# Swapping the two operands of the samples' value matmuls in the attention stage of a decoder step

## The reference, cut to what matters

```python
o_cmp = jnp.einsum('bkgtn,bnkd->btkgd', p_cmp, vc.astype(F32))      # 255 compressed blocks
...
o_sel = nsa_selected(qg, k_sel, v_sel, top_idx, top_ok, qpos, rel_bias)  # 16 blocks chosen out of the 4096 past positions
...
o_win = nsa_window(qg, kw_all, ...)                                  # the last 512 positions
...
o = gates[:, :, 0] * o_cmp + gates[:, :, 1] * o_sel + gates[:, :, 2] * o_win
```

## Time and profile before

| | share of the span | instructions |
|---|---|---|
| PE (matmul) | 91% | 13788 |
| PEld (weight load) | 77% | 13788 |
| VectorE | 44% | 2381 |
| ScalarE | 19% | 1184 |
| GpSimd | 11% | 322 |

### The profile page before, as it was taken

The page is one execution under the profiler, slowest core; times in us unless marked ns, Lnnn a source line. Parts: engine busy times, 40 slices in busy tenths (PEclk is TensorE's granted clock), DMA queues, the critical chain, the costliest instruction groups (busy, mean ns, idle before and its releaser), DMA issues. The chain is left out here.

```text
span 2642.2 us, 38209 instructions
## 1 busy us (share of the span) xinstructions
PE 2404.4 (91%) x13788; PEld 2026.4 (77%) x13788; DVE 1167.7 (44%) x2381; ACT 498.3 (19%) x1184; POOL 294.0 (11%) x322
## 2 busy tenths in 40 slices
PE   7996999689798999999989969986988989999997
PEld 6873999567597788888868759985767868888885
DVE  1933665445457544101038246654544675440012
ACT  1013111223421211000010221112342221110001
POOL 0600000000222011001006000000003121110010
PEclk9996999789899999999989979987999989999998
DMA  6204998244210222522042159962440103215210
GB/s 193 80 27 136 266 267 217 67 129 121 73 42 18 80 80 80 144 64 64 0 125 64 32 162 268 263 165 82 139 124 18 42 17 112 80 48 126 65 32 34
DMA packets 335879, 273.89 MB, mean 104 GB/s; under 512 B 53569, under 2 KB 331458, under 8 KB 335482
## 3 DMA queue, kind: packets, MB, share of 16 engines
q1 hardware_dynamic: 272424, 203.30, 27.9%
q10 hardware_dynamic: 63314, 68.70, 9.8%
HBM read 262.07 MB, written 18.17 MB: 106 GB/s over the span
## 5 line engine op out<-in xcount | busy, mean ns | idle before, releaser
L2658 PE MATMUL psum<-ff,HT 128*128 128x272 f32 x1536 | 353.3, 392 | 0.0
L447 PE MATMUL psum<-xT,ring 128*128 128x272 f32 x1408 | 327.5, 396 | 21.5 <-PEq L169 21.5
L2658 PEld LDWEIGHTS psum<-ff,HT 128*128 128x128 f32 x1536 | 291.8, 190 | 60.2
L447 PEld LDWEIGHTS psum<-xT,ring 128*128 128x128 f32 x1408 | 269.9, 192 | 78.1 <-issue 22.0
L1156 DVE STREAM_TRANSPOSE turned<-ring 128x1536 f32<-128x1536 f32 x128 | 222.7, 1765 | 117.6 <-PE psum L1035 78.8
L1035 PE MATMUL psum<-turned,W 128*128 128x128 f32 x2048 | 249.1, 281 | 0.0
L1035 PEld LDWEIGHTS psum<-turned,W 128*128 128x128 f32 x2048 | 241.2, 197 | 0.0
L2504 PE MATMUL psum<-yT,HT 128*128 128x272 f32 x896 | 215.1, 397 | 0.0
L2504 PEld LDWEIGHTS psum<-yT,HT 128*128 128x128 f32 x896 | 172.4, 193 | 36.0
L1025 PE MATMUL psum<-yT,turned 128*128 (+1 forms) x1024 | 123.5, 275 | 32.6 <-DVE turned L1156 32.6
L1025 PEld LDWEIGHTS psum<-yT,turned 128*128 128x128 f32 x1024 | 122.7, 196 | 34.0 <-issue 32.0
(11 more groups left out here) (526 smaller groups left out, 3336.4 us busy)
## 6 DMA issues: line engine op xcount, KB each, us to landing
ring<-in_cache_nsa_kv SPq DMA_DIRECT2D x256, 192.0 KB, 5.5
ring<-in_cache_nsa_kv ACTq DMA_DIRECT2D x256, 192.0 KB, 5.6
ring<-in_w_up SPq DMA_DIRECT2D x32, 1024.0 KB, 5.5
ring<-in_cache_nsa_kv SPq DMA_DIRECT2D x384, 64.0 KB, 1.9
HT<-in_w_down SPq DMA_DIRECT2D x12, 2048.0 KB, 9.0
ring<-in_w_in SPq DMA_DIRECT2D x20, 1024.0 KB, 5.2
ring<-in_cache_nsa_kv ACTq DMA_DIRECT2D x128, 64.0 KB, 2.2
HT<-in_w_out SPq DMA_DIRECT2D x8, 1024.0 KB, 5.2
```

Of the source, the lines that this page charges most:

```text
L447: last = pe.matmul(psum[0:w.shape[1], 2 * (t % 3) + h, 0:HALF], w, S.xT[:, k, h * HALF:(h + 1) * HALF], start=(k == 0), stop=(k == KT - 1))
L2658: last = pe.matmul(out[h], down[t % 3][:, k, :], f[:, k, x], start=(k == 0), stop=(k == FT - 1))
```

## The change

In `sample_third` the two operands of each matmul change places: the values (pages, window, compressed blocks, new tokens) are now stationary, 128 positions by 128 channels, and the 16 columns of probabilities move. The sum has its 128 channels on partitions and a sample's 16 rows as columns, so that all 8 samples fit in 128 columns of bank 7. The copies out of PSUM (L1496), the waits for them (L1419, L1483), the 8 transposes at the end (L1485) and the buffer `o_s` go away. VectorE's placement into `yT` now waits for the last half of the last sample (`s.part`) where it waited for the transposes. The counts of matmuls, and the DMAs, are the same.

```diff
@@ -1364,7 +1364,6 @@
     half = NPG // 2
     vsel = ring_view(S, 2, half, P)
     vwin = sb("vwin", [P, 4, P], ctx=ctx)
-    o_s = sb("o_s", [16, NB, P], ctx=ctx)
     units = [(i, h, br) for i in range(QT) for br in range(3) for h in (0, 2, 1, 3)]
     N = len(units)
     sc = sb("sc", [P, 3, 512], ctx=ctx)
@@ -1374,7 +1373,7 @@
     coef = sb("coef", [P, N], ctx=ctx)
     o = sb("o", [P, QT, 256], ctx=ctx)
     names = ("scored", "added", "step", "maxed", "exped", "turned", "pt_copied", "pv", "summed", "coef", "o_turned", "o_copied",
-             "pages0", "pages1", "pages_act0", "pages_act1", "window", "part", "s_copied", "s_turned", "placed")
+             "pages0", "pages1", "pages_act0", "pages_act1", "window", "part", "placed")
     with stage(nc, "att", *names) as (block, s):
         pages, pages_act = (s.pages0, s.pages1), (s.pages_act0, s.pages_act1)
         by_sp = 12
@@ -1413,23 +1412,21 @@
                 part, third = n // 3, n % 3
                 b, h = part // 2, part % 2
                 cols = slice(16 * b, 16 * b + 16)
-                o = psum[0:16, 6 + b % 2, 0:P]
+                o = psum[:, 7, cols]
                 if h == 0 and third == 0:
-                    if b >= 2:
-                        pe.wait_ge(s.s_copied, b - 1)
-                    pe.matmul(o, S.pt_new[:, 0, cols], S.kv_s[:, 3 * P:4 * P], start=True, stop=False)
-                    pe.matmul(o, S.pt_new[:, 1, cols], S.kv_s[:, 5 * P:6 * P], start=False, stop=False)
+                    pe.matmul(o, S.kv_s[:, 3 * P:4 * P], S.pt_new[:, 0, cols], start=True, stop=False)
+                    pe.matmul(o, S.kv_s[:, 5 * P:6 * P], S.pt_new[:, 1, cols], start=False, stop=False)
                     for j in range(2):
                         m = P - j
-                        pe.matmul(o, S.pt_cmp[0:m, j, cols], S.vc[0:m, j, b, :], start=False, stop=False)
+                        pe.matmul(o, S.vc[0:m, j, b, :], S.pt_cmp[0:m, j, cols], start=False, stop=False)
                     pe.wait_ge(s.window, 16 * b + 16)
                     for j in range(4):
-                        pe.matmul(o, S.st_win[:, j, cols], vwin[:, j, :], start=False, stop=False)
+                        pe.matmul(o, vwin[:, j, :], S.st_win[:, j, cols], start=False, stop=False)
                 if third == 0:
                     pe.wait_ge(pages[h], 16 * by_sp * (b + 1))
                     pe.wait_ge(pages_act[h], 16 * (half - by_sp) * (b + 1))
                 for t in range(half * third // 3, half * (third + 1) // 3):
-                    last = pe.matmul(o, S.st_sel[:, half * h + t, cols], vsel[:, h, t, :], start=False, stop=(h == 1 and t == half - 1))
+                    last = pe.matmul(o, vsel[:, h, t, :], S.st_sel[:, half * h + t, cols], start=False, stop=(h == 1 and t == half - 1))
                 if third == 2:
                     last.then_inc(s.part, 1)
 
@@ -1480,10 +1477,6 @@
             for n in range(N - lag, N):
                 sample_third(n)
             pe.wait_ge(s.summed, N)
-            pe.wait_ge(s.s_copied, NB)
-            for b in range(NB):
-                last = pe.transpose(psum[:, 7, 16 * b:16 * b + 16], o_s[:, b, :], C["ident"][0:16, 0:16])
-            last.then_inc(s.s_turned, 1)
             for i in range(QT):
                 for c in range(2):
                     last = pe.transpose(psum[:, (6, 0)[c], i * P:i * P + P], o[:, i, c * P:c * P + P], C["ident"])
@@ -1491,10 +1484,6 @@
 
         @block.scalar
         def _(act):
-            def copy_out(b):
-                act.wait_ge(s.part, 2 * b + 2)
-                act.copy(o_s[:, b, :], psum[0:16, 6 + b % 2, 0:P]).then_inc(s.s_copied, 1)
-
             def fetch_rest(part):
                 if part >= 2:
                     act.wait_ge(s.part, part - 1)
@@ -1509,8 +1498,6 @@
                     act.wait_ge(s.maxed, n + 1)
                     x = sc[:, n % 3, 0:width(n)]
                     act.activation(x, x, ACT.Exp, bias=nmax[:, n:n + 1], accum_out=esum[:, n:n + 1]).then_inc(s.exped, 1)
-                if n - lag - 2 in range(6, 6 * NB, 6):
-                    copy_out((n - lag - 2) // 6 - 1)
                 if n >= 1:
                     m = n - 1
                     act.wait_ge(s.turned, m + 1)
@@ -1519,8 +1506,6 @@
                     w = 31 if width(m) == 31 else P
                     x = slice(0, P if w == 31 else width(m))
                     act.copy(pt[0:w, m % 3, x], psum[0:w, 2 + m % 2, x]).then_inc(s.pt_copied, 1)
-            for b in range((N - lag - 2) // 6, NB):
-                copy_out(b)
             act.wait_ge(s.o_turned, 1)
             for c in range(2):
                 act.copy(S.yT[:, 4 + c, 0:SEQ], psum[:, (6, 0)[c], :]).then_inc(s.o_copied, 1)
@@ -1559,7 +1544,7 @@
                     else:
                         dve.wait_ge(s.summed, m)
                         dve.scalar_tensor_tensor(out, src, coef[:, m:m + 1], out, ALU.mult, ALU.add).then_inc(s.summed, 1)
-            dve.wait_ge(s.s_turned, 1)
+            dve.wait_ge(s.part, 2 * NB)
             rows = psum[:, 7, 0:P].rearrange("p (b k g t) -> p b k g t", b=NB, k=KVH, g=GRP)
             for k in range(KVH):
                 for g in range(GRP):
```

## The result

The changed kernel takes 2808.96 us, the median of 4 runs (2805.81 to 2821.52), against 2642.7 for the kernel before, now the median of 4. The ratio is 1.0636, with a 95% interval of 1.0614 to 1.0659: 6.4% slower. The profiled execution took 2805.81 us, 161.8 more than that of before. The granted clock is 0.873 on average over the span, where it was 0.946.

What follows compares the result with a forecast made beforehand. The prediction took PE's issue of records to bound the attention stage. 2644.0 us plus 172.4 for both low-clock stages and 0.4 for what follows gave 2816.8, stated as 2817 us, 6.5% slower, with a range of 2765 to 2832.

Steps and rivals of the forecast that it cites:

- The bound: First attention stage: PE's issue of records bounds it, 0.110 us from one page record to the next.
- The record at full clock, 0.111: Samples' matmuls: swapped operands cost 0.111 us a record, so 640 records cost 1 us more a layer.
- Changes of shape, 4 us a layer: Steps between samples' records and transposes: like shapes save 0.17 us at 32 units, net 4 us a layer at full clock.
- the 1.1 of the copies: Stage's end: final transposes and the copy ahead of them, about 1.1 us a layer on the path, go away.
- The clock: Attention stages: 16 streamed columns leave the clock low to the stage's end; 2817 us, chance 0.80.
- The rival that the clock holds: Attention stages: PE without idle time keeps or regains its clock; 2634 us, chance 0.07.
- a late return of the clock: Late in the attention stages: transposes, values and scores bring the clock back; 2765 to 2800 us, chance 0.10.
- that nothing moves: Attention stages: the low clock lasts as long as now and shape changes stay; 2644 us, chance 0.02.
- The record at the low clock, 0.213: Samples' matmuls: 0.213 us a record at the low clock, 136.3 us for 640 records a layer.
- The stage, 241.4 us: First attention stage at the low clock: parts sum to 235.5 us, with start and waits 241.4, against 155.2 today.
- The same difference in both layers, +86.2: Both attention stages: each takes 86.2 us longer, +172.4 together.
- What follows, +0.4, bounds -3 and +6: Stage after attention, layer one: starts at the low clock, +0.4 us once; bounds -3 and +6 us for both layers.

Runs made afterwards that it cites:

- the run without waits: The changed kernel with 128 moving columns for the first sample, 16 for the others, and pages and window fetched once a stage: 2790.24 us.
- The form with both operands 128 wide: The changed kernel with all 128 probability columns moving for every sample: 2637.26 us, ratio 0.9987.
- three buffers: The changed kernel with 128 moving columns, and the kernel before, each with three half-sample buffers and two windows: 2615.86 us and 2620.42 us.
- four samples of 128 columns: The changed kernel with 128 moving columns for samples 0 to 3, and 64 or 16 for samples 4 to 7: 2747.18 us or 2739.07 us.
- a moving width of 64 columns: The changed kernel with 128 moving columns for the first sample, 64 for the others, and pages and window fetched once a stage: 2692.45 us.
- the kernel that had them throughout: The changed kernel with 64 moving columns for every sample: 2811.32 us in one execution.

## Why the prediction was right

*The bound.* Right. The stage was bound by PE's issue of records before, and is after: no idle time ahead of the page records, 600.49 to 603.02 for twelve of them.

*The record at full clock, 0.111.* Right as far as it can be seen. The changed kernel's stage ran there for its first 2 us only, ahead of any page record. In the run without waits the first ten page records with 16 moving columns still had the full clock, and took 0.112 each (533.33 to 534.45). The form with both operands 128 wide takes 0.113 in a row of 44, against 0.109 before.

*Changes of shape, 4 us a layer.* Right in mechanism (0.11 for 0.20 at the third's end), but too large: it left out the step at the entry to a third, 0.165 for 0.119. With three buffers, where neither order has a second low stretch, the stages differ by 2.1 us in the first layer and by -0.1 in the second, not by 4 and the 1.1 of the copies. And it is a gain at full clock, at which the changed kernel ran none of its page records.

*The clock.* Right, and its reason too, but the rows of before were thinner than the 0.80 put on them. The fall in the midst of busy records is real: the same 24 records come eight times in the first layer's stage, and in ten of the thirteen traces of this case the clock falls just behind one of the eight (in the kernel with 128 columns from 1.00 at 336 to 0.55 in the window from 339). But it is never more than one of the eight, and none in the changed kernel. That the one trace at hand showed it was in part luck. The return with 128 moving columns and not with 32 also fits another reading, since the narrow records filled 3.4 us and the wide ones 6.4: the time that PE was busy. No run parts the two there. The experiments show it on the stage itself, by the width alone (128 against 64 and 16) and without any wait (the fall at 535). The rival that the clock holds while PE is never idle is refuted by the same fall. That rival's time is what the Trainium skill, page "TensorE: Matmul & The Clock Gate", section "Loop structure matters more than you think", would have given: matmuls kept back to back stay warm. The traces disagree, with 3.00 of 3.00 us busy ahead of the fall. Of the other rivals, a late return of the clock is excluded by the window at 745 (it would have given 2765 to 2800 us), and that nothing moves by the result. (The first rival's condition was also mis-sized: a gain of 5.1 us a layer is lost when the low clock lasts 10 us longer, at half its length, and not 8.)

*The record at the low clock, 0.213.* Right: 0.211 and 0.2125.

*The stage, 241.4 us.* Slightly too much. To the end of the last transpose it took 738.67 + 1.95 - 503.54 = 237.1 us, 4.3 less. Summed from start to start in the trace, the units' transposes and values with 31 keys took 14.3 us, not 15.4 and 2.2: the twelve records ahead of the one at 603.02 step by 0.211 up to and with it, so there is no extra for a change of shape there. The idle time at the start was 5.1, not 5.9; the prompt's values 33.3, not 34.1; the scores 26.3, not 26.7. The 2 us for smaller gaps are not there by themselves, but the other transposes took 18.7, not 17.0, and the samples' records 137.4, not 136.3. The last eight transposes took 1.95, not 1.8.

*The same difference in both layers, +86.2.* It was +81.9 and +86.5. The changed stages are equal (238.19 and 238.74), as forecast. The stages before were not (156.30 and 152.23), and I had read only the first. The low clock comes a second time in both, and lasts longer in the first layer. It is 13.7 us there and 3.4 in the second. Windows of the kernel before, first and second layer, each some 45 us behind the stage's start:

```profile
551.00:554.00 3.00, 3.00 (x15) 1.75 (x13) 1.38 (x6) 0.60 (x2) 0.00 (x0) 0.50 0.34 92
1851.00:1854.00 3.00, 3.00 (x25) 1.90 (x22) 2.03 (x9) 0.80 (x3) 0.00 (x0) 1.00 0.44 129
```

The 10.2 us more at half speed cost 5, about the 4.1 by which the layers differ. In the second layer the sum's excess (241.4 against 237.6) and this slip cancelled each other. The same stretch lasts half as long with 128 moving columns (0.94 in the window from 554 above), which is 3.4 of that kernel's gain of 5.8 us in its first stage.

*What follows, +0.4, bounds -3 and +6.* Missed: outside the two stages the execution is 6.6 us shorter, 2.5 of it before the first stage, 3.6 between the two and 0.5 after. All that runs ahead of the first stage is the same code in every kernel here, and the first record of its scores stood at 506.01 us in the profiled execution of before, at 503.54 with the change and at 510.26 with four samples of 128 columns. So a few us in either direction belong to the single execution. Part of it is seen: the fall at 409 is not there after the change. The +0.4 for the next stage's start was too small: from the prompt's last transposes to the delta-rule stage's L1770 (L1785 before) it takes 784.58 - 738.67 = 45.91 us in the first layer and 45.65 in the second, against 45.00 and 45.38. The bounds should have taken this scatter in; the sum came out at 172.8 where 161.8 were measured, 11.0 too much: 7.0 here and 4.3 in the first layer's stage, less 0.3 in the second's.

## What to carry over

Before turning the operands of a chain of matmuls around so that fewer columns move, price its records at both clock levels, and look for stretches of the trace where PE is busy with as narrow a stream: if the clock falls there, even in some executions only, the chain can pull down everything interleaved with it, here also the prompt's transposes and values. A kernel that waits a little and streams wide can be faster than one that never waits and streams narrow, and taking the waits away is worth more than their own length where the clock falls behind them. When two stages are forecast from one, read the other too, and give the rest of the program the scatter of an execution.

## What the hardware showed that I had not expected

At a moving width of 64 columns the same code ran once at full clock through a whole stage (136.73 us) and once at the low clock (219.97 us). And a wait of 0.83 us stood ahead of a fall at 64 columns, where one of 1.05 us passed at 128 without a trace. Whether the wait was its cause is open; at 128 columns falls stood behind waits of 1.78 and 1.87 us, and one of 2.48 passed. Where the clock was lost, 64 columns mostly did not bring it back: not in 242 us of the kernel that had them throughout, though in one stretch of another (at 631, 96 us after the fall) it did come back.

A record with both operands 128 wide steps by 0.113 us at full clock, where 16 stationary columns and 128 moving ones step by 0.109 and 128 stationary and 16 moving ones by 0.112. A narrow operand on one side only buys next to nothing; on both sides it buys, at the low clock, a factor of 7 (0.213 to 0.029).
